# Forget gate, query and output gate columns: six pairs of blocks with seven half-block products each, in place of eight, in a two-layer hybrid encoder

## The reference

```
z = x @ w_in      # columns: q-down | kv-latent | rope key | hq | hf | hi | hg | cu | cv | gates A, B, C
logf = logaddexp(log(lb), log1p(-lb) + log_sigmoid(hf));  kk = (1 - lb) * sigmoid(-hf);  qq = hq;  vv = hi
o_h  = HGRN2 recurrence(qq, kk, vv, logf)               # per token, 4 heads of 128
y_b  = (rms_norm(o_h) * silu(hg)) @ w_pb
y_a  = latent attention;   y_c = (gelu(cu) * spatial_mix(layer_norm(gelu(cv)))) @ w_pc
m    = sig(gA)*y_a + sig(gB)*y_b + sig(gC)*y_c;          x = LN(alpha*x + m @ w_o)
gate, up = x @ w_up;                                     x = LN(alpha*x + (silu(gate)*up) @ w_down)
```

## Time and profile before

| | us |
|---|---|
| median of 3 runs | 2048.5 |
| lowest and highest | 2044.56, 2049.47 |
| the profiled execution | 2049.53 |
| its span, first to last instruction | 2047.7 |
| TensorE busy in the span | 2019.0 |
| DVE busy, ACT busy | 1271.6, 834.9 |
| mean granted TensorE clock | 0.995 |

### The profile page before, as it was taken

The page is one execution under the profiler, slowest core; times in us unless marked ns, Lnnn a source line. Parts: engine busy times, 40 slices in busy tenths (PEclk is TensorE's granted clock), DMA queues, the critical chain, the costliest instruction groups (busy, mean ns, idle before and its releaser), DMA issues.

```text
span 2047.7 us, 37990 instructions
## 1 busy us (share of the span) xinstructions
PE 2019.0 (99%) x15612; PEld 1942.8 (95%) x15612; DVE 1271.6 (62%) x2074; ACT 834.9 (41%) x1471; POOL 82.1 (4%) x96
## 2 busy tenths in 40 slices
PE   7999999999999999999999999999999999999999
PEld 6899999988999999999998999989889999999998
DVE  5444645775269998863465365367734789888433
ACT  5232134544344555552253221344443454556422
POOL 1000000000002000000010000010000100000100
PEclk9999999999999999999999999999999999999999
DMA  5232212312132233333333222132212322333321
GB/s 175 74 83 62 63 50 66 89 54 63 42 104 78 73 102 100 104 96 87 97 92 78 76 62 68 40 97 58 64 41 71 95 83 73 104 104 107 90 87 52
DMA packets 287915, 163.97 MB, mean 80 GB/s; under 512 B 8984, under 2 KB 279552, under 8 KB 287744
## 3 DMA queue, kind: packets, MB, share of 16 engines
q1 hardware_dynamic: 283712, 152.07, 26.4%
q0 software_dynamic: 3552, 8.36, 1.3%
q10 hardware_dynamic: 480, 1.13, 0.2%
HBM read 156.86 MB, written 4.66 MB: 79 GB/s over the span
## 4 chain that ended last, share of the span: by engine, by line
PE 96%; DVE 2%; ACT 1%; issue 0%; DMA 0%; DVEq 0%; ACTq 0%
PE acc L792 52%; PE ring L1173 13%; PE acc L778 7%; PE ring L814 4%; PE acc L1173 3%; PE ring L898 2%; PE ring L1052 2%; PE ring L1071 1%; PE acc L814 1%; PE ring L1060 1%; PE ring L1122 1%; PE ring L1104 1%; PE ring L1389 1%; PE ring L935 0%; PE ring L949 0%; PE ring L925 0%
## 5 line engine op out<-in xcount | busy, mean ns | idle before, releaser
L2200 DVE TENSOR_TENSOR wlo<-raw,whi 128x1024 fp32r<-128x1024 f32 (+2 forms) x324 | 306.3, 951 | 308.8 <-ACT whi L1515 308.0
L1515 ACT ACTIVATE whi<-raw 128x1024 fp32r<-128x1024 f32 (+2 forms) x324 | 269.3, 839 | 490.0 <-PE acc L792 400.4
L792 PE MATMUL acc<-xh,whi 128*128 128x272 f32 x1376 | 311.3, 308 | 4.6 <-DVE xl L2200 4.3
L792 PE MATMUL acc<-xl,whi 128*128 128x272 f32 x1376 | 286.3, 289 | 0.0
L792 PE MATMUL acc<-xh,wlo 128*128 128x272 f32 x1376 | 286.3, 289 | 0.0
L792 PEld LDWEIGHTS acc<-xh,whi 128*128 128x128 f32 x1376 | 218.8, 191 | 19.7 <-issue 15.3
L792 PEld LDWEIGHTS acc<-xl,whi 128*128 128x128 f32 x1376 | 218.6, 190 | 0.0
L792 PEld LDWEIGHTS acc<-xh,wlo 128*128 128x128 f32 x1376 | 217.6, 190 | 0.0
L1173 PE MATMUL ring<-xb,whi 128*128 128x272 f32 x768 | 147.0, 289 | 2.5 <-ACT xf L1515 2.2
L792 PE MATMUL acc<-hh,whi 128*128 128x272 f32 x704 | 146.0, 289 | 0.0
L792 PE MATMUL acc<-hl,whi 128*128 128x272 f32 x704 | 145.2, 288 | 0.0
(11 more groups left out here) (468 smaller groups left out, 4171.8 us busy)
## 6 DMA issues: line engine op xcount, KB each, us to landing
raw<-in_w_in_dram SPq DMA_DIRECT2D x104, 512.0 KB, 3.7
raw<-in_w_up_dram SPq DMA_DIRECT2D x88, 512.0 KB, 3.9
raw<-in_w_down_dram SPq DMA_DIRECT2D x32, 512.0 KB, 4.0
raw<-in_w_o_dram SPq DMA_DIRECT2D x16, 512.0 KB, 3.9
raw<-in_w_down_dram SPq DMA_DIRECT2D x16, 384.0 KB, 3.3
raw<-in_w_pc_dram SPq DMA_DIRECT2D x16, 256.0 KB, 2.7
raw<-in_w_pb_dram SPq DMA_DIRECT2D x16, 256.0 KB, 2.7
raw<-in_w_pa_dram SPq DMA_DIRECT2D x16, 256.0 KB, 2.7
```

Of the source, the lines that this page charges most:

```text
L792: last = pe.matmul(dst[:, b * 512:b * 512 + HALF], w[:, c:c + P], x[:, k0 + a, b * HALF:(b + 1) * HALF], start=start and a == 0 and q == 0 ...
L1515: return act.activation(dst, src, ACT.Copy)
L2200: return dve.tensor_tensor(out, a, b, op)
```

## The change

The twelve units of the front stage become six pairs, `FRONT = 6`: pairs 0 and 1 are hf, 2 and 3 hq, 4 and 5 hg. Each has seven products of 12 matmuls (`PRODUCTS`, numbered 0 to 6; product 5.4 below is number 4 of pair 5, and product number q counts through all 42). Products 0, 2, 4 and 6 go into one bank (half of `acc[0]`, the halves alternate by pair), 3 and 5 into `acc[1][0:512]`, 1 into `acc[1][512:1024]`. ACT copies four running sums to `gs` (`front_keep`), DVE adds three quarters of the output together (`front_lin`), and ACT copies the last quarter (`front_last`). The raw outputs of hf lie in `K`, of hq in `Q`, of hg in `o`; the sigmoids now read SBUF, two blocks at once (`front_gates`), a pair later. The weight operands use the four half slots of `whi` and `wlo` (`front_slot`); the last two products use slots 2 and 3, so that `whi[0]` is free for `U_MC`. The x sums are made, split and put in `y`, `yr`, `fs`, `fb` during the hi stage (`front_sums`, `front_hi`, `front_lo`, four each). SP's loads for pair p + 2 wait for the last low part of pair p (`front_read`).

```diff
+FRONT = 6
...
+    def front_slot(q):
+        return q % 4 if q < OF_PAIR * FRONT - 2 else 2 + q % 2
+    def front_used(q):
+        return next((r + 1 for r in range(q - 1, -1, -1) if front_slot(r) == front_slot(q)), 0)
...
+    gs_flat = gs[:, :, :].rearrange("p b t -> p (b t)")
+    front_kept = [gs_flat[:, HALF * i:HALF * (i + 1)] for i in range(4)]
+    def front_banks(p):
+        return acc[0][:, 512 * (p % 2):512 * (p % 2) + 512], acc[1][:, 0:512], acc[1][:, 512:1024]
+    def front_out(p):
+        return (K, Q, o)[p // 2][:, 2 * (p % 2):2 * (p % 2) + 2, :]
...
+            def front_read(n):
+                p = (n - RAW - U_HF) // 2
+                if 0 <= p < FRONT:
+                    sp.wait_ge(*in_front("wt_lo", l, OF_PAIR * (p + 1)))
+                    passed(sp, "sp")
+                return not 0 <= p < FRONT
...
+        def front_product(layer, p, i):
+            a, b, c = front_banks(p)
+            q = OF_PAIR * p + i
+            pe.wait_ge(*in_front("wt_lo", layer, q + 1))
+            if p == 0 and i == 1:
+                pe.wait_ge(*tile_freed("hi4", layer))
+            elif p > 0 and i == 1:
+                pe.wait_ge(*in_front("pr_lin", layer, 3 * (p - 1) + 1))
+            elif p > 0 and i == 3:
+                pe.wait_ge(*in_front("pr_lin", layer, 3 * (p - 1) + 3))
+            if p == 0 and i in (2, 3, 4, 6):
+                pe.wait_ge(*in_front("xb_lo", layer, {2: 2, 3: 3, 4: 3, 6: 4}[i]))
+            if p > 1 and i == 0:
+                pe.wait_ge(*in_front("pr_sig", layer, p - 1))
+            if i in (2, 4, 5, 6):
+                pe.wait_ge(*in_front("pr_kept", layer, 4 * p + {2: 1, 4: 2, 5: 3, 6: 4}[i]))
+            dst = (a, c, a, b, a, b, a)[i]
+            w1, w2 = front_weights(q)
+            first = i in (0, 1, 3)
+            for k in range(4):
+                for r, (w, part) in enumerate(((w1, 0), (w1, 1), (w2, 0))):
+                    last = pe.matmul(dst[:, 0:HALF], w[:, k * P:(k + 1) * P], front_block(i, part)[:, k, :],
+                                     start=first and k == 0 and r == 0, stop=k == 3 and r == 2, skip_group_check=True)
+            last.then_inc(*inc("pr_done"))
...
+            between = {(0, 3): [(vector_columns, ())], (0, 6): [(spatial_weights, ())], (2, 3): [(mix, (0,))], (2, 6): [(mix, (1,))],
+                       (3, 3): [(mix, (2,))], (3, 6): [(mix, (3,)), (mix, (4,))]}
+            tile("front", l)
+            for p in range(FRONT):
+                for i in range(OF_PAIR):
+                    front_product(l, p, i)
+                    for step, args in between.get((p, i), ()):
+                        step(l, *args)
+            pe.wait_ge(*in_front("pr_lin", l, 3 * FRONT))
...
+            def front_weight_hi(q):
+                p, i = divmod(q, OF_PAIR)
+                name = PRODUCTS[i]
+                if name in WEIGHT_TERMS:
+                    act.wait_ge(*in_front("wt_sum", l, 3 * p + WEIGHT_TERMS[name]))
+                else:
+                    loaded(l, U_HF + 2 * p + (i == OF_PAIR - 1))
+                if q < 4:
+                    act.wait_ge(*used_unit(l, U_HI + (2 if q < 2 else 3)))
+                else:
+                    act.wait_ge(*in_front("pr_done", l, front_used(q)))
+                copy(front_weights(q)[0], front_source(q)).then_inc(*inc("wt_hi"))
...
+            def front_keep(p, n):
+                act.wait_ge(*in_front("pr_done", l, OF_PAIR * p + KEPT[n] + 1))
+                if p > 0:
+                    act.wait_ge(*in_front("pr_lin", l, 3 * (p - 1) + (1, 3, 2, 2)[n]))
+                copy(front_kept[n], front_banks(p)[1 if n == 2 else 0][:, 0:HALF]).then_inc(*inc("pr_kept"))
+            def front_last(p):
+                act.wait_ge(*in_front("pr_done", l, OF_PAIR * (p + 1)))
+                ins = copy(front_out(p)[:, 1, 0:HALF], front_banks(p)[0][:, 0:HALF]).then_inc(*inc("pr_sig"))
+            def front_gates(p):
+                k = 2 * (p % 2)
+                act.wait_ge(*in_front("pr_sig", l, p + 1))
+                act.wait_ge(*in_front("pr_lin", l, 3 * (p + 1)))
+                if p < 2:
+                    act.activation(F[:, k:k + 2, :], K[:, k:k + 2, :], ACT.Sigmoid).then_inc(inc("f_sig", 2)[0], 2)
+                    act.wait_ge(*at("f_sig", l, 2 * k + 2))
+                    act.activation(K[:, k:k + 2, :], K[:, k:k + 2, :], ACT.Sigmoid, scale=-1.0).then_inc(inc("f_sig", 2)[0], 2)
+                elif p > 3:
+                    act.activation(og[:, k:k + 2, :], o[:, k:k + 2, :], ACT.Sigmoid).then_inc(inc("og_sig", 2)[0], 2)
+            next_hi(l, U_HI + 2)
...
+            front_weight_hi(0)
+            front_weight_hi(1)
+            for c in (4, 0, 1, 2, 3):
                 if c < 4:
                     act.wait_ge(*group_ready(f"hi{c}", l))
                     copy(vhi[:, c, :], gbank(f"hi{c}")[:, :]).then_inc(*group_free(f"hi{c}"))
+                    if c == 0:
+                        front_weight_hi(3)
                 else:
                     act.wait_ge(*used_unit(l, U_HI + 3))
                     copy(vhi[:, c, :], acc[tile_at["hi4"] % 2][:, 0:512]).then_inc(*tile_free("hi4"))
...
+                    front_weight_hi(2)
+            for p in range(FRONT):
+                q = OF_PAIR * p
+                front_keep(p, 0)
+                front_weight_hi(q + 4)
+                front_weight_hi(q + 5)
+                if p > 0:
+                    front_gates(p - 1)
+                front_keep(p, 1)
+                front_weight_hi(q + 6)
+                front_keep(p, 2)
+                if p < FRONT - 1:
+                    front_weight_hi(q + 7)
+                    front_keep(p, 3)
+                    for i in (8, 9):
+                        front_weight_hi(q + i)
+                    front_last(p)
+                    front_weight_hi(q + 10)
+                else:
+                    act.wait_ge(*in_front("pr_done", l, q + 3))
+                    next_hi(l, U_MC)
+                    front_keep(p, 3)
                     act.wait_ge(*at("cm_mixed", l, 5))
+                    act.wait_ge(*in_front("pr_done", l, q + 5))
                     copy(ych[:, :, :], u[:, :, :]).then_inc(*inc("yc_hi"))
+                    front_last(p)
+            act.wait_ge(*in_front("pr_done", l, OF_PAIR * FRONT))
+            next_hi(l, U_MC + 1)
+            front_gates(FRONT - 1)
...
+            def front_weight_sum(p, n):
+                r = front_raw(p)
+                w11, w21, w12, w22 = (r[:, 512 * c:512 * c + 512] for c in range(4))
+                if n == 0:
...
+                    dve.wait_ge(*in_front("wt_lo", l, OF_PAIR * p + 1))
+                    earlier = r.rearrange("p (b c) -> p b c", b=2)[:, :, 0:512]
+                    later = r[:, 1024:2048].rearrange("p (b c) -> p b c", b=2)
+                    tt(earlier, later, earlier, ALU.subtract).then_inc(*inc("wt_sum"))
+                elif n == 1:
+                    dve.wait_ge(*in_front("wt_sum", l, 3 * p + 1))
+                    if p > 0:
+                        dve.wait_ge(*in_front("wt_lo", l, OF_PAIR * (p - 1) + 3))
+                    tt(rs[:, 0:512], w22, w11, ALU.subtract).then_inc(*inc("wt_sum"))
+                else:
+                    dve.wait_ge(*in_front("wt_sum", l, 3 * p + 2))
+                    dve.wait_ge(*in_front("wt_lo", l, OF_PAIR * p + 2))
+                    tt(w21, w21, rs[:, 0:512], ALU.subtract).then_inc(*inc("wt_sum"))
+            def front_weight_lo(q):
+                dve.wait_ge(*in_front("wt_hi", l, q + 1))
+                hi, lo = front_weights(q)
+                tt(lo, front_source(q), f32(hi), ALU.subtract).then_inc(*inc("wt_lo"))
...
+            front_weight_lo(0)
+            front_weight_sum(0, 0)
+            front_weight_lo(1)
+            front_weight_sum(0, 1)
+            front_weight_sum(0, 2)
+            front_lo(F_S1)
+            front_lo(F_S2)
+            front_lo(F_S3)
+            front_weight_lo(2)
+            front_weight_lo(3)
+            front_lo(F_S4)
+            after_hi(3)
+            for p in range(FRONT):
+                q = OF_PAIR * p
+                for i in (4, 5):
+                    front_weight_lo(q + i)
+                front_lin(p, 0)
+                front_weight_lo(q + 6)
+                if p in (1, 2):
+                    after_hf(2 * p - 2)
+                    after_hf(2 * p - 1)
+                    if p == 1:
+                        layer_vectors(1)
+                elif p == 3:
+                    dve.wait_ge(*(at("cu_gelu", l - 1, 4) if l > 0 else tile_freed("cu3", l)))
+                    mixed(1)
+                elif p == 4:
+                    mixed(3)
+                elif p == 5:
+                    after_hg(0)
+                    after_hg(1)
+                if p < FRONT - 1:
+                    front_weight_lo(q + 7)
+                    front_weight_sum(p + 1, 0)
+                    front_weight_lo(q + 8)
+                    front_weight_sum(p + 1, 1)
```

(45 more changed lines are left out.)

162 lines of the change are left out of this document (111 added, 51 removed).

## The result

| | before | after |
|---|---|---|
| median, us (5 runs each) | 2048.5 | 2060.74 |
| lowest and highest | 2044.56, 2052.58 | 2058.41, 2067.64 |
| profiled execution | 2049.53 | 2058.41 |
| front stage, layer 0 and 1 | 78.46, 78.45 | 81.75, 83.27 |

A forecast was written before the change was run, and what follows sets the result against it. TensorE bounds the kernel, busy 2019.0 of 2047.7 us. Per layer, 68.94 without waits plus 10.27 of waits and restarts gives 79.21 against 78.46; two layers +1.5, predicted 2050 against the median 2048.5, range 2043 to 2057.

The forecast's parts named there:

- What goes: Front stage: 576 matmuls a layer become 504, so without waits 68.94 us in place of 78.46, 9.52 less.
- Wait 1: Product 0.2 waits for the first kept sum, behind weight and ring copies on ACT: 1.25 us.
- Wait 2: Product 0.4 waits for its low part, behind an x low part and two normalisation chunks on DVE: 1.17 us.
- Wait 3: Product 1.4 waits for kept sum 1, behind the table load and pair 0's sigmoids on ACT: 1.66 us.
- Wait 5: Product 5.4 waits for kept sum 1, behind product 5.5's weight copy, which needs the slot 5.3 reads: 2.26 us.
- Wait 6: Product 5.5 waits for kept sum 2, behind 5.6's weight copy, which waits for the end of 5.4: 1.26 us.
- Wait 7: The first merge gate, after the front stage, waits for the last front_lin on DVE: 0.51 us.
- Wait 4: Products 2.0, 2.1 and 2.2 wait behind DVE's list of scalings, spatial weights and weight sums: together 1.52 us.
- And it stays: Front stage: small work between products (five mixes, turned vectors and weights) stays at 5.38 us a layer.
- Elsewhere I see nothing: Outside the front stage no cost: DVE ends its backlog some 4 us into gc0, before the tree needs it.
- Rival B: The clock falls around products 5.4 and 5.5, once per layer, +6.6 us on top: 2056.6; chance 15%.
- Rival A: ACT's and DVE's lists keep up; waits 1, 2, 4 and 7 go, stage 74.36 us, kernel 2040; chance 15%.

The follow-up runs named there:

- experiment 9: The changed kernel with only the two overlooked waits mended (104 tiles a layer, layer_vectors(0) early): 2051.72 us, ratio 1.0018.
- experiment 10: The kernel of experiment 8 with the turned spatial weights moved on DVE to the end of pair 1: 2030.34 us, ratio 0.9922.
- experiment 7: The changed kernel with kept sum 0 ahead of three ring copies on ACT and two normalisations later on DVE: 2060.0 us, ratio 1.0069.
- experiment 3: The changed kernel with ACT's kept sums 1 and 2 ahead of the weight copies of products 5.5 and 5.6: 2051.97 us, ratio 1.0025.
- experiment 4: The changed kernel with an unused one-column sigmoid on ACT in the hi stage, so the table loads there: 2056.98 us, ratio 1.0050.
- experiment 8: The changed kernel with experiment 1, experiment 2, experiment 4, experiment 7, a later sigmoid to K and a new pair 5 order: 2034.18 us, ratio 0.9937.
- experiment 2: The changed kernel with layer_vectors(0) ahead of pair 0's first front_lin on DVE, not at the pair's end: 2054.22 us, ratio 1.0044.
- experiment 1: The changed kernel with one more tile number in each layer, 104 in place of 103, ahead of dn0: 2059.38 us, ratio 1.0062.
- Experiment 6: The kernel before, without pairs, with two added TensorE waits in each layer, at hf3 and hq0: 2059.76 us, ratio 1.0063.

## Why the prediction was wrong, step by step

- **What goes**: 68.94 without waits. Right to 1 us: 79.13 in experiment 9 less its nine waits (8.56) and their restarts (0.6 to 0.7) is 69.9, and experiment 10 reaches 70.47 with 0.53 of wait. The pace of 1.513 held: between two starts, a product with no interruption takes 1.49 to 1.52 (experiment 10, products 4.4 to 5.3). One that comes behind a mix, the turned weights or a short hold takes 1.6 to 1.7, and I had added 0.08 behind the named waits alone. All 42 in experiment 10 take 65.3 without the wait, 63.56 by the prediction; the small work between them takes 4.7 in place of 5.38. That is the 1.0 over.
- **Wait 1**, 1.25: 1.02. **Wait 2**, 1.17: 1.08. **Wait 3**, 1.66: 1.77. **Wait 5**, 2.26: 2.15. **Wait 6**, 1.26: 1.16. **Wait 7**, 0.51: 0.33. Right, and so are their causes: experiment 7 took away 1 and 2, experiment 3 took 5 and 6, experiment 4 took 3 down to 0.36, and 7 is gone in experiment 8.
- **Wait 4**, 1.52: 1.04 in experiment 9, at the three products named, and too large by a half; hidden under a slow stretch in the profiled execution after.
- **"And it stays"**, the small work between products at 5.38, with no wait of its own. This step failed. I moved the turned vectors and the spatial weights with their duration and did not ask what they wait for in the new order. `spatial_weights` needs the bank that `layer_vectors(0)` gives back, and that stood behind all of DVE's pair 0: 2.42 a layer (experiment 2).
- **"Elsewhere I see nothing"**. This failed too. An odd number of tiles puts the last of layer 0 and the first of layer 1 into one accumulator: 1.75 and a restart (experiment 1). With line 933 that makes 2 x 2.5 + 1.8 = 6.8 us that the sum had at nothing, the larger part of the 10.7 by which the medians differ from the forecast (12.2 against 1.5). It could be read in the diff, in the `+ 1` of `TILES`.
- **The clock.** The likeliest case had none of it, and this failed as well. It is the rest of the miss: 3.9 us between the medians, 5.4 by the ratio, by difference and not measured by itself. Experiment 9 agrees in kind: with the 6.8 us of overlooked waits gone, 10.0 go by the ratios. Rival B had the mechanism and gave 2056.6, but looked at 5.4 and 5.5 alone and at 3.3 us a fall. Falls came behind the pair of waits 2.42 and 1.77 that I had half overlooked, at the boundary, and only sometimes behind 5.4; one loses 1.7, seldom 3.4, and costs less where it lies over another wait. Experiment 6 shows that added waits bring them about. Why one wait is followed by a fall and the same wait in the other layer isn't stays open.
- **Rival A** (lists keep up): no, as the named waits show. But the lists have the room: experiment 10 keeps 8.0 of the 9.5 us a layer, by order, one more tile number and an early table load.
- **Rival C** (the table load drains): no. The timeline of ACT after has the sigmoid 0.01 behind the load's end:

```profile
125.52 1.28 ACT L1961 ACT_TABLE_LOAD   x1
126.81 1.11 ACT L1961 ACTIVATE F<-K 128x1088 f32<-128x1088 f32 x1
128.02 1.11 ACT L1963 ACTIVATE K<-K 128x1088 f32<-128x1088 f32 x1
129.03 0.38 ACT L1617 ACTIVATE gs<-acc 128x272 f32<-128x272 f32 x1
```

The Trainium skill (ScalarE: Activation LUTs, What ACT_TABLE_LOAD costs) gives 1283 ns, which this row bears out, and a drain of about 1380 ns on top, which it does not. The next two rows also give the price I lacked: a sigmoid over 1088 columns takes 1.11, with the next start 1.0 to 1.2 behind, so the copy's was the right neighbour.
- **Rival D** (loads late): no wait for `raw` in the trace.

By sizes, in the profiled executions. The stages: my +1.5, then 2 x 2.5 for line 933, 5.1 of slow clock (1.7 and 3.4), less 2 x 1.76 for wait 4 and its restarts, which these stretches hid; the other named waits were 0.6 shorter than said and the matmuls 0.6 longer, per layer. That makes 8.1, and the windows show 8.11. Between the stages +3.07: 1.8 for the wait at cu0 and 1.7 for the clock behind it, with 0.5 the other way that I did not trace. Behind them -2.57, of which 1.7 is clock and the rest not traced; ahead +0.09. So the two overlooked waits are 6.8 us here, and the slow stretches behind waits lose 6.8 too but cost some 3.3, since they hid wait 4.

## What to carry to other kernels

When work moves to another place in a list, ask two things of each piece: how long it takes, and whose release it waits for (ring banks and alternating buffers above all, whose count the change may make odd). Where the tensor engine was full, two waits with 6 us of work between them cost 1.7 times their length here; for one alone the 1.3 times between the medians can't be told from its bare length. A slow stretch in one profiled execution isn't yet a finding, since before has them too. And before a change with fewer matmuls is given up, read the waits one by one, since all but one of these went, most by order and the rest by a tile number and an early table load.
